# Taking the filler matmuls out of a hybrid-mixer kernel's attention, state-space heads and last mixer

## The reference, cut to what matters

```
# attention of the first block, per head
s = einsum('bcqhd,bckhd->bhcqk', qc, kb) * hd ** -0.5 + bias
p = softmax(where(valid, s, min));  o = einsum('bhcqk,bckhd->bcqhd', p, vb)
# state-space heads of the first block
decay  = exp(where(causal, seg, -inf))
y_diag = einsum('bclsg,bclsgm,bcsgmp->bclgmp', cb, decay, xdt)
# last mixer: stick-breaking attention, per head
z = q k^T;  log_not = log_sigmoid(-z);  suffix = cumsum(log_not, reverse) - log_not
out = exp(log_sigmoid(z) + suffix) @ v
```

## Time and profile before

| what | value |
|---|---|
| median of 3 executions | 2891.28 us (2886.98 to 2892.08) |
| the profiled execution, its own time | 2889.05 us |
| span of the profile, first to last instruction | 2887.2 us |
| mean granted TensorE clock | 0.972 of 2.4 GHz |
| PE busy | 2722.0 us, 12266 matmuls |
| DVE, ACT, POOL busy | 1033.5, 1042.4, 1082.7 us |

### The profile page before, as it was taken

One profiled execution on the slowest core, in us unless ns is written; L12 is line 12 of the kernel. 1 busy time (PEld: TensorE's weight loads), 2 busy tenths in 40 slices (PEclk: granted clock), 3 DMA queues, 4 the chain that ended last, 5 costly groups with the idle time before them and its releaser, 6 DMA issues.

```text
span 2887.2 us, 33813 instructions
## 1 busy us (share of the span) xinstructions
PE 2722.0 (94%) x12266; PEld 2170.3 (75%) x12266; DVE 1033.5 (36%) x1540; ACT 1042.4 (36%) x1484; POOL 1082.7 (37%) x494
## 2 busy tenths in 40 slices
PE   8999999979899999888889999999999889999998
PEld 6888888744688888666777778888778567888886
DVE  3212228247422122667455642122432322321214
ACT  4312333334432222455344452222342443422233
POOL 4444444400244444233333334444344302444443
PEclk9999999989999999999899999999999999999999
DMA  4222222300122223122000022322222101322323
GB/s 146 98 98 95 98 99 78 118 0 1 59 93 96 98 93 101 61 71 73 30 20 25 23 80 94 102 95 95 81 88 94 37 0 51 102 95 95 99 98 102
DMA packets 61707, 222.50 MB, mean 77 GB/s; under 512 B 6704, under 2 KB 6832, under 8 KB 61488
## 3 DMA queue, kind: packets, MB, share of 16 engines
q1 hardware_dynamic: 60928, 218.07, 22.6%
q10 hardware_dynamic: 688, 3.15, 0.3%
HBM read 219.09 MB, written 2.10 MB: 77 GB/s over the span
## 4 chain that ended last, share of the span: by engine, by line
PE 86%; DVE 8%; ACT 3%; issue 2%; DMA 0%; SPq 0%; DVEq 0%; ACTq 0%
PE ps L345 15%; PE ps L347 15%; PE ps L346 15%; PE ps L370 7%; PE ps L371 7%; PE ps L372 7%; PE ps L1898 2%; PE ps L608 1%; PE ps L1321 1%; PE ps L1323 1%; PE ps L1322 1%; PE ps L1409 1%; PE ps L1383 1%; DVE sum_sq L446 1%; PE ps L688 1%
## 5 line engine op out<-in xcount | busy, mean ns | idle before, releaser
L2128 POOL TENSOR_TENSOR w_lo<-raw,w_hi 128x1024 fp32r<-128x1024 f32 x405 | 986.4, 2437 | 1484.8 <-ACT w_hi L411 1484.7
L345 PE MATMUL ps<-x_hi,w_hi 128*128 128x512 f32 x1896 | 744.6, 393 | 21.9 <-DMA const<-in_constants_dram 13.5
L346 PE MATMUL ps<-x_lo,w_hi 128*128 128x512 f32 x1896 | 739.4, 390 | 0.0
L347 PE MATMUL ps<-x_hi,w_lo 128*128 128x512 f32 x1896 | 739.0, 390 | 0.0
L411 ACT ACTIVATE w_hi<-raw 128x1024 fp32r<-128x1024 f32 x405 | 425.3, 1051 | 548.0 <-PE ps L372 361.1
L345 PEld LDWEIGHTS ps<-x_hi,w_hi 128*128 128x128 f32 x1896 | 356.7, 188 | 104.5 <-DMA const<-in_constants_dram 13.5
L346 PEld LDWEIGHTS ps<-x_lo,w_hi 128*128 128x128 f32 x1896 | 356.9, 188 | 74.9 <-issue 1.9
L347 PEld LDWEIGHTS ps<-x_hi,w_lo 128*128 128x128 f32 x1896 | 356.9, 188 | 74.6
L370 PE MATMUL ps<-mid_hi,w_hi 128*128 128x512 f32 x896 | 351.8, 393 | 13.1 <-DVE mid_lo L1829 13.1
L371 PE MATMUL ps<-mid_lo,w_hi 128*128 128x512 f32 x896 | 350.3, 391 | 0.0
L372 PE MATMUL ps<-mid_hi,w_lo 128*128 128x512 f32 x896 | 350.1, 391 | 0.0
(11 more groups left out here) (305 smaller groups left out, 3050.3 us busy)
## 6 DMA issues: line engine op xcount, KB each, us to landing
raw<-in_units_dram SPq DMA_DIRECT2D x406, 512.0 KB, 3.2
h<-in_x_t_dram SPq DMA_DIRECT2D x4, 512.0 KB, 7.0
toep<-in_rel_table_dram ACTq DMA_DIRECT2D x1, 2048.0 KB, 9.3
out_dram<-h SPq DMA_DIRECT2D x4, 512.0 KB, 5.4
p_f<-in_p_t_dram ACTq DMA_DIRECT2D x2, 512.0 KB, 3.6
const<-in_constants_dram SPq DMA_DIRECT2D x1, 832.0 KB, 9.3
vec<-in_vectors_dram SPq DMA_DIRECT2D x1, 133.5 KB, 2.2
```

What stands on the lines that cost most here:

```text
L345: nc.tensor.matmul(out, hi, x_hi[:, k, :], start=(k == 0), stop=False)
L346: nc.tensor.matmul(out, hi, x_lo[:, k, :], start=False, stop=False)
L347: last = nc.tensor.matmul(out, lo, x_hi[:, k, :], start=False, stop=(k == DK - 1))
L2128: nc.gpsimd.tensor_tensor(w_lo[:, n % W_SLOTS, :], raw[:, n % RAW_SLOTS, :], w_hi[:, n % W_SLOTS, :].bitcast(F32), ALU.subtract).then_inc( ...
```

## The change

It removes the function `pe_keep_warm` and its seven calls. 3 + 4 + 16 + 3 + 8 + 16 + 8 = 58 filler matmuls are no longer issued, or 116 matmul records and as many weight loads. No wait, no semaphore and no other instruction changes, and the order of all that remains is the same on every engine.

```diff
@@ -602,11 +602,6 @@
-        def pe_keep_warm(bank, count):
-
-            for _ in range(count):
-                nc.tensor.matmul(ps[:, bank, :], ones, const[:, 0:4, :], start=True, stop=True)
@@ -696,14 +691,12 @@
                 turn_probs(pair, 1)
-                pe_keep_warm(3, 1)
                 values(pair, 1)
...
             scores(0, 1)
-            pe_keep_warm(3, 3)
             with pe.Fori(0, 3) as i:
@@ -765,7 +758,6 @@
                     broadcast(i, t + 2)
-                    pe_keep_warm(5, 1)
                     y_head(i, t)
@@ -1869,11 +1861,9 @@
             pe.wait_ge(s_free, w.bank + 4)
-            pe_keep_warm(7, 3)
             pe_tile_norm(pe, w)
             pe_tile_norm(pe, w)
             pe.wait_ge(s_tln, w.batches)
-            pe_keep_warm(7, 8)
@@ -1890,7 +1880,6 @@
                 pe.wait_ge(s_mlo, i * 2 + w.mids)
-                pe_keep_warm(6, 4)
@@ -1898,7 +1887,6 @@
-                pe_keep_warm(7, 2)
```

## The result

| | before | changed |
|---|---|---|
| median of 18 executions | 2890.16 us (2886.49 to 2895.78) | 2895.41 us (2894.34 to 2904.82) |
| ratio | | 1.0025, 95% interval 1.0017 to 1.0032 |
| span of the profile | 2887.2 us | 2892.8 us |
| mean granted clock | 0.972 | 0.962 |
| PE busy, matmuls | 2722.0 us, 12266 | 2681.8 us, 12150 |

A forecast was written before the change was run, and what follows sets the result against it. PE was taken to bound the kernel, holding 86% of the chain of waits. Attention 4.8, heads 1.4 and last mixer 1.5 sum to +7.7 us: 2889.05 becomes 2896.8, as a median 2899.0, range 2888 to 2910.

The forecast's parts named there:

- Attention, +4.8: Start of the attention: transposes still wait for DVE, but transposes, scores and part of the values run slow, +4.8 us.
- The single fillers: Four fillers between the attention's transposes and values: they only become idle time behind ACT's copy, 0 us.
- State-space heads, -8.2 and +9.6: Loop of heads: fillers off the path save 8.2 us, four spells at 1.2 GHz cost 9.6, net +1.4.
- the price of one spell: Loop of heads: a 6.7 us spell at 1.2 GHz loses 3.4, less 1.0 of filled idle time: 2.4 us.
- The gain: Loop of heads at full clock: two heads take 7.94 us instead of 8.84, 7.2 plus 1.0 us saved.
- Last mixer, +1.5: Last mixer: slow first scores +1.4, norms +0.5, pairs -0.4, groups of four 0; sum +1.5 us, bounds -1 and +4.
- 1.4 + 0.5: Last mixer: +1.4 us for ACT's later start behind slow scores, +0.5 for the norms without three fillers ahead.
- the -0.4 of the pairs: Last mixer, fillers behind L1898: PE goes on 0.1 us earlier in each of four rounds, -0.4 us.
- The first rival: Loop of heads: the clock holds, sum -1.9 us, median 2889.4, no change that can be told; chance 0.20.
- The second: Loop of heads: DVE never waits for a broadcast, two heads take 7.4 us, -7.4 in all, median 2883.9; chance 0.07.
- The third: Loop of heads: half the heads stay at 1.2 GHz, +13.6 us there, +19.9 in all, 2911; chance 0.13.
- The rule of the Trainium skill: Ties the clock's fall to PE idle gaps, not rows; by it the loop stays at 2.4 GHz, sum -1.9 us.

The follow-up runs named there:

- the two-filler pair: Two kernels, each with two fillers per state-space head instead of the one in the kernel before: 128 rows deep 2903.61 us, 16 rows deep 2932.30, against 2890.75.
- the run with every second filler: Kernel before, with the state-space heads' filler kept only in heads t = 1 and 3, the other eight taken out: 2883.44 us against 2890.75, ratio 0.9973.
- the repeat for the start of the attention: Kernel before without the three fillers behind the attention's first two scores, measured again with more rounds: 2896.18 us against 2889.51, ratio 1.0017.
- its first run: Kernel before without the three fillers behind the attention's first two scores, 5 executions: 2899.53 us against 2890.19, ratio 1.0034.

## Why the prediction was right

The forecast was 2899.0 us, +7.7; measured were 2895.41 us, which is +5.3 by the medians and +7.2 us by the ratio (4.9 to 9.2). The forecast started from a median of 2891.28 over three executions, 1.1 us above that of the 18. By its steps:

1. *Attention, +4.8.* Measured +5.4 in the changed kernel's trace, and +4.0 and +7.5 with this edit alone. The mechanism is as written: the transposes began when DVE released them, at 0.50, took 2.39 us, and the values 3.38 (of 2.37 and 4.53; I had put 3.6). The first pair accounts for 4.3 of the 5.4 us; the other 1.1 in later pairs were not in the sum. The single fillers: 0 forecast, 0.9999 measured.
2. *State-space heads, -8.2 and +9.6.* Both halves are real: 1.35 us of idle PE before every second y_head, 3.37 us for the other head, and five spells at 0.50. Their sum was -1.5 us and not +1.4. The spells were five, not four, but only one of them lasted 6.6 us; the other four lasted about half that, as the stretch at 0.50 in the earlier trace rows already did, and half of a shorter spell is lost. The term that was off most is the price of one spell: 2.4 us, taken from the attention's 6.7 us spell. The gain was too large as well: at full clock two heads take 8.16 us, not 7.94, because the head with a gate takes 4.79 (704.36 to 709.15) and not 4.57. That makes the gain without a spell about 8 x (8.84 - 8.16) + 1.0 = 6.4 us instead of 8.2, and the price of one spell about (6.4 - 1.5) / 5 = 1.0 us. Both are estimates: no run holds the clock without any filler in the loop.
3. *Last mixer, +1.5.* Measured +3.3, at the upper side of the bounds. ACT's first L1956 came 37.47 us into the mixer instead of 35.09, +2.4 where my terms gave 1.4 + 0.5 = 1.9: I had counted the first head's K as ready 0.7 us earlier, which the slower norms ahead of it used up (they took 15.69 us instead of 14.10, and the scores came 32.80 us into the mixer, 32.70 before). I let ACT's two passes over the first head cover the second head's scores, and ACT waited 0.48 us for them. And the -0.4 of the pairs did not come: behind the first sums the rounds took 0.3 us longer.
4. The errors of 2 and 3 cancel in part: -2.9 and +1.8, with +0.6 in the attention and -1.6 in stretches that the change does not touch (-0.4 and -1.2), 7.7 becomes the 5.6 us between the two spans. The total was nearer than its terms, and that is luck.

The first rival, that the clock holds in the loop, is refuted by the stretches at 0.50 and by the two-filler pair, in which the clock fell without idle time. The second, that the heads go at DVE's pace, by the idle time of DVE in front of its exponents (L991) in the changed kernel, 0.41 us that the broadcast ends; and with the clock held, in the run with every second filler, two heads take 8.16 us and not the 7.4 of that rival:

```profile
715.43 1.13 DVE L991 TENSOR_SCALAR decay<-ps,bias_c 128x128 f32<-128x128 f32 x4 [0.41 <-PE ps L738]
```

The third, a loop that sticks at 1.2 GHz, did not come: after each fall the clock was back within 7 us, with y_heads and broadcasts running. The rule of the Trainium skill ("TensorE: Matmul & The Clock Gate", "Why this matters for your kernels") that idle gaps cost the clock agrees with the last mixer of these traces, where 15.34 us of idle PE stood before slow matmuls. In the attention 5.07 us of idle PE stood before slow matmuls too, but there the clock was at 0.50 already from 565.0 on, ahead of that gap. It is not enough for the loop of heads, where gaps of 1.35 us were: a gap of 1.45 us between matmuls of 128 rows kept the clock in the attention, and in the loop a 16-row broadcast stands beside the gap.

The parts measured one by one come to about +11.6 us by their ratios (+4.9, -0.3, +1.2, +5.8), each uncertain by 3 us, and the whole to +7.2 by its own. That agrees within the intervals and no better, and it takes the repeat for the start of the attention; with the +9.8 of its first run the parts would come to 16.5, which does not agree. By the stretches of the traces the parts are +4.0 or +7.5, -2.5 and +3.3, and the whole is +5.6.

## What to carry to other kernels

A matmul that nobody reads has two prices that must be read apart: the time that it holds PE, which is zero in a wait and full outside of one, and what it does to the clock of the matmuls behind it. Look in front of every stretch at the lower clock for a wait of PE; a filler that reaches nearly to the end of the wait pays, one that stops 4 us short of it doesn't, and one on the path was worth about what it cost here (all sixteen of the loop out: ratio 1.0004). Where removing it and keeping it both cost, keep it in the iterations in which PE would wait anyway.

## What the runs showed of the hardware that I had not expected

PE can be busy for all of 50.00 us and still lose its full clock: with two 16-row fillers in each head the granted clock had a mean of 0.76, with two 128-row fillers of the same 512 columns it was 1.00. I had expected that few rows weaken the hold, from the earlier trace rows, but not a clock that goes down and up once in nearly every head, all through the second part of the loop.

The clock's changes do not fall at the same place of the program in every execution. The first scores of the attention took 2.39 us in eight of the thirteen traces and 4.08 to 4.60 in the other five, with the same instructions ahead of them, and the same edit cost 4.0, 5.4 and 7.5 us in three traces. A single profile of such an edit is good for the mechanism and not for its size to a few microseconds.
